# Hyena long convolution: the inverse transform over folded spectra, and the first output tile between the inverse transforms

## The chip, the cores and the metric

One core of a Trainium2 chip runs the whole program in one launch. The metric is the device time in microseconds (us) of that core, median of the runs. The engines named here are TensorE (PE; its weight loads PEld), VectorE (DVE), ScalarE (ACT), GpSimd (POOL) and the queue of SyncE (SP) that starts most transfers.

## The reference, cut to what matters

Four layers over 256 latent and 256 context tokens of width 1024; layer 1 is a Hyena mixer, and the change lies in it alone:

```python
def _bidir_long_conv(u, h_fwd, h_bwd, skip):
    l = u.shape[1]
    n = 2 * l
    filt = jnp.concatenate([h_fwd, jnp.zeros_like(h_fwd[:1]), h_bwd[:0:-1]], axis=0)
    uf = jnp.fft.rfft(u.astype(jnp.float32), n=n, axis=1)
    ff = jnp.fft.rfft(filt, n=n, axis=0)
    y = jnp.fft.irfft(uf * ff[None], n=n, axis=1)[:, :l]
    return (y + u.astype(jnp.float32) * skip.astype(jnp.float32)).astype(u.dtype)

def _hyena_mixer(...):
    u = _dwconv(h @ w_in + b_in, conv_w, conv_b)
    x0, x1, v = jnp.split(u, 3, axis=-1)
    ...
    v = _bidir_long_conv(v * x1, h_fwd, h_bwd, skip)
    return (v * x0) @ w_out + b_out
```

It runs on the latent and on the context tokens with the same weights. Everything is float32.

## The kernel before, in words

The transform is taken at 256 odd frequencies as matrix products. A frequency k and its mirror 255-k are handled as a pair: even and odd input samples are transformed apart (128 frequencies each), and a sum and a difference of the two ("butterfly") give the 256 spectra. The long convolution is cut into four windows w = 0 to 3: w = 2*hf + st, where hf is the half of the 1024 channels and st is latent or context. For each window:

- `turn_x1v(w)` (PE, L1044) turns the gated input by 8 transposes; ACT copies it out.
- `forward(w, im)` (PE, L1060) makes the even and odd parts; ACT copies the odd part (`odd_part`).
- `butterflies(w, im)` (DVE, L1895, L1897): 2 instructions for the real and 2 for the imaginary part.
- `products(w, b)` (DVE, L1909 to L1917): for each half b of the frequencies 4 products and 2 sums, written to `y_spec`; 12 instructions a window.
- `inverse(w)` (PE, L1075): for each of 4 channel blocks 4 float32 products of 128 channels by 256 samples (real and imaginary, b = 0 and 1) into one accumulation. A float32 product is recorded as two MATMUL instructions, so a window has 32.
- `gate(w)` (DVE, L1925): 2 instructions multiply the result, from PSUM, by x0 into `x1v`.
- ACT (L1455) copies it into `u_hi` in 4 pieces, POOL (L2029) makes `u_lo` in 4 pieces and raises `c_lo` at each.

Windows 0 and 1 go through forward and products inside the last four input tiles (t = 8 to 11 of `hyena_in`), where PE is busy with the projection; windows 2 and 3 come after the last one. There DVE's written order is: the products (1,1), then for w = 2 and 3 the butterflies, the products and `gate(w - 2)`, then `gate(2)` and `gate(3)`. PE's is forward(2), inverse(0), turn 3, forward(3), inverse(1), inverse(2), inverse(3), and then the output projection `x_phase`. `products(w, 0)` of w = 2 and 3 waits for inverse(w - 2), as it writes over its `y_spec`.

The output projection has four weight tiles. Its first one (t = 0) takes channels 0 to 511, which are windows 0 and 1, for 4 blocks of 128 tokens: per block a bias product and 12 MATMULs. Before the first of these it waits for `c_lo` of 8. The second tile takes channels 512 to 1023 and waits for `c_lo` of 16. The weights of a tile are loaded by SP once the tile three before is done, and split into `w_hi` (ACT L1155) and `w_lo` (DVE L1517). Each engine runs its list in order; waits are on semaphores, set by hand.

Of the kernel before, what the change touches and what calls it, by code (L numbers as in the profile page):

```python
# [21 lines left out]
P = 128  # L22
# [77 lines left out]
def constants():  # L100

    f = np.float32
    out = {}

    def rope(dh):
        axis = dh // 2
        inv = np.power(f(10000.0), -np.arange(0, axis, 2, dtype=f) / f(axis)).astype(f)
        t = np.arange(SEQ)
        ang = np.concatenate([(t // GRID_W).astype(f)[:, None] * inv[None],
                              (t % GRID_W).astype(f)[:, None] * inv[None]], axis=-1)  # L110
        half = dh // 2
        cos, sin = np.zeros((P, SEQ), f), np.zeros((P, SEQ), f)
        for p in range(P):
            cos[p] = np.cos(ang[:, p % half]).astype(f)
            sin[p] = np.sin(ang[:, p % half]).astype(f)

        rot = np.zeros((P, P), f)
        for p in range(P):
            if p % dh < half:
                rot[p + half, p] = -1.0  # L120
            else:
                rot[p - half, p] = 1.0
        return cos, sin, rot

    cos, sin, rot = rope(A_DH)
    out["k_rope_a"] = np.concatenate([cos, sin, rot], axis=1)
    cos, sin, rot = rope(C_DH)

    mats = [rot]
    for kv in range(C_KV):  # L130
        dup = np.zeros((P, P), f)
        for p in range(P):
            dup[C_DH * kv + p % C_DH, p] = 1.0
        mats += [dup, (rot.astype(np.float64) @ dup).astype(f)]
    mask = np.zeros((2, P, TOK), f)
    for b in range(2):
        q = b * P + np.arange(P)[:, None]
        mask[b, :, :SEQ] = np.where(np.abs(np.arange(SEQ)[None, :] - q) <= 128, 0.0, -1e30)
    out["k_rope_c"] = np.concatenate([cos, sin] + mats + [mask[0], mask[1]], axis=1)

    pick = np.zeros((P, 2), f)
    for p in range(P):
        if p % 32 < 2:
            pick[p, p % 32] = 1.0
    out["k_ident"] = np.concatenate([np.eye(P, dtype=f), 1.0 - np.eye(P, 1, dtype=f), pick], axis=1)


    t = np.linspace(0.0, 1.0, SEQ, dtype=f)[:, None]
    omega = (f(2.0 * math.pi / SEQ) * np.arange(SEQ, dtype=f)).astype(f)
    bands = np.linspace(1e-4, 15, 16, dtype=f)  # L150
    ang = (omega[:, None] * bands[None, :]).astype(f)
    z = np.concatenate([t, np.cos(ang), -np.sin(ang)], axis=-1).astype(f)
    out["k_zt"] = np.ascontiguousarray(z.T)
    rates = np.abs(np.linspace(math.log(1e-2) / 0.3, math.log(1e-2) / 1.5, D, dtype=f))
    by_parity = np.concatenate([np.arange(0, SEQ, 2), np.arange(1, SEQ, 2)])
    out["k_decay"] = np.exp(-t * rates[None, :]).astype(f)[by_parity]

    pos = np.arange(SEQ, dtype=np.float64)[:, None]
    th = 2 * np.pi * ((pos * (2 * np.arange(SEQ)[None, :] + 1)) % (2 * NFREQ)) / (2 * NFREQ)
    out["k_dft"] = np.concatenate([np.cos(th[:, :P]), -np.sin(th[:, :P])], axis=1)[by_parity].astype(f)

    order = np.concatenate([np.arange(P), SEQ - 1 - np.arange(P)])
    ang = th.T[order]
    out["k_idft"] = (2.0 / NFREQ * np.concatenate([np.cos(ang), -np.sin(ang)], axis=0)).astype(f)
    return out


def build(nc, a, out):

    es = ExitStack()
    with es:
# [67 lines left out]
        def region(*items):  # L242

            got, at = [], M0
            for name, shape, off in items:
# [21 lines left out]
            ("decay", [P, 2, D], None), ("f_w4", [P, D], None), ("f_w", [P, 4 * FW], None), ("f_b", [P, 3], None))  # L267
        ZT, SK = region(("f_in", [P, SEQ], 4 * 16 * TOK), ("skip_row", [P, D], None))
        YS, VX, IF = region(("y_spec", [P, 2, 4, 512], 4 * (16 * TOK + 5 * D + 12 * P)),
                            ("x1v_tok", [P, 2, 2, 512], None), ("idft", [P, 4, SEQ], None))  # L270

        MG = [None] * 4
        MG += region(*((f"mod_unit{s}", [P, KT, TW], 8 * D * (s - 4)) for s in range(4, 8)))
# [6 lines left out]
        def rope_mat(m):  # L280
# [44 lines left out]
        f_odd, c_odd = sem("f_odd"), sem("c_odd")  # L325
        c_turned, c_vt, c_fwd, c_fly, c_prod, c_y = (sem("c_turned"), sem("c_vt"), sem("c_fwd"), sem("c_fly"),
                                                     sem("c_prod"), sem("c_y"))
        c_inv, c_gated, c_hi, c_lo = sem("c_inv"), sem("c_gated"), sem("c_hi"), sem("c_lo")
        dve_chain = sem("dve_chain")

# [252 lines left out]
        def _(pe):  # L583
# [129 lines left out]
                                  start=True, stop=True)  # L713
                    last.then_inc(u_turned, 1)

            def x_phase(k, X, Y, arrive, free):

                n0, nt, NB = XFIRST[k], XTILES[k], XN[k]
                kts = [sum(TILES[n0 + t][3] for t in range(x)) for x in range(nt)]
# [23 lines left out]
                for t in range(2 * nt - 2):  # L743
                    n, (h, tt) = n0 + t, divmod(t, nt)
                    nr, kt = TILES[n][3], kts[tt]
                    pe.wait_ge(lo_ready, n + 1)
                    if k % 2 == 0 and tt == 1:
                        for j in range(nr):
                            arrive(kt + j)
                            for b in range(NB):  # L750
                                ins = step(n, h, b, j, kt, False, j == nr - 1)
                                if j == nr - 1:
                                    finished(h, b, ins)
                            if j == nr // 2 - 1:
                                for x in MID.get(n, []):
                                    reduce_mod(x)
                    else:
                        for b in range(NB):
                            if tt == 0:
                                enter(h, b)  # L760
                            for j in range(nr):
                                if h == 0 and b == 0:
                                    arrive(kt + j)
                                ins = step(n, h, b, j, kt, not has_bias(k) and tt == 0 and j == 0, tt == nt - 1 and j == nr - 1)
                            if tt == nt - 1:
                                finished(h, b, ins)
                            if b == NB // 2 - 1:
                                for x in MID.get(n, []):
                                    reduce_mod(x)
                    ins.then_inc(tile_done, 1)  # L770
                    for x in END.get(n, []):
                        reduce_mod(x)

# [289 lines left out]
            def long_conv():  # L1063
                def inverse(w):
                    pe.wait_ge(c_y, 4 * (w + 1))
                    if w == 0:
                        pe.wait_ge(tab_in, TAB_AT[1] + 16)
                        pe.wait_ge(c_fly, 8)
                    elif w == 1:
                        pe.wait_ge(c_vt, 8)  # L1070
                    else:
                        pe.wait_ge(c_gated, 2 * (w - 1))
                    for c in range(4):
                        for j in range(4):
                            last = mm(y_bank(w, c // 2)[:, (c % 2) * SEQ:(c % 2 + 1) * SEQ], YS[:, w % 2, j, c * P:(c + 1) * P],  # L1075
                                      IF[:, j, :], start=(j == 0), stop=(j == 3))
                    last.then_inc(c_inv, 1)

                def spectra(w):
                    forward(w, 0)  # L1080
                    forward(w, 1)

                spectra(2)
                inverse(0)
                turn_x1v(3)
                spectra(3)
                inverse(1)
                inverse(2)
                inverse(3)

            for i in range(DEPTH):
                N = NL[i]
                n0, q0 = FIRST["in", i], PAIR0["in", i]
                if KIND[i] == 1:
# [3 lines left out]
                    for t in range(2, 12):  # L1098
# [5 lines left out]
                        if t in (8, 10):  # L1104
                            forward(t // 2 - 4, 0)
                            forward(t // 2 - 4, 1)
                    long_conv()
                    arrive = lambda k: pe.wait_ge(c_lo, 8 * (k // 4 + 1))
                    free = lambda b: ((c_fly, 16),)
                else:  # L1110
                    if i > 0:
                        first_tiles(n0, q0, 2 * i, (N, TOK))
                    issued = 0 if KIND[i] == 2 else 3 if i == 0 else 4
# [18 lines left out]
                    arrive = lambda k, G=ahead(GROUPS, i): pe.wait_ge(ao_lo, G + k + 1)  # L1132
                    free = lambda b, i=i: ((p_evac, ahead(NH, i) + NH[i]),) if b < 2 else ((ao_lo, ahead(GROUPS, i) + GROUPS[i] - 3 + b),)

                x_phase(2 * i, UH, UL, arrive, free)

                n0, q0 = FIRST["up", i], PAIR0["up", i]
                first_tiles(n0, q0, 2 * i + 1, (N, N))
# [362 lines left out]
        def _(dve):  # L1501
# [319 lines left out]
            def hyena_in():  # L1821
# [4 lines left out]
                for t in range(12):  # L1826
# [47 lines left out]
                        butterflies(t // 2 - 4, 1)  # L1874
                    if t >= 8:
                        products(t // 2 - 4, t % 2)

            def filter_taps(x):

# [19 lines left out]
            def products(w, b):  # L1899
# [12 lines left out]
                tt(re, im, BF[:, 2 + b, s], ALU.mult).then_inc(c_prod, 1)  # L1912
                tt(im, im, BF[:, b, s], ALU.mult).then_inc(c_prod, 1)
                dve.wait_ge(c_prod, n + 3)
                tt(y_re, y_re, re, ALU.subtract).then_inc(c_y, 1)
                dve.wait_ge(c_prod, n + 4)
                tt(y_im, y_im, im, ALU.add).then_inc(c_y, 1)  # L1917

            def long_conv():
                def gate(w):  # L1920
                    hf, st = divmod(w, 2)
                    dve.wait_ge(c_inv, w + 1)
                    for m in range(2):
                        cs, t = slice(4 * hf + 2 * m, 4 * hf + 2 * m + 2), slice(st * SEQ, (st + 1) * SEQ)
                        tt(XV[:, cs, t], y_bank(w, m).rearrange("p (c t) -> p c t", c=2), X0[:, cs, t],  # L1925
                           ALU.mult).then_inc(c_gated, 1)

                dve.wait_ge(z_conv, 3 * KT)
                for w in (2, 3):
                    butterflies(w, 0)  # L1930
                    butterflies(w, 1)
                    products(w, 0)
                    products(w, 1)
                    gate(w - 2)
                gate(2)
                gate(3)

# [202 lines left out]
```

## Time and profile before

| | |
|---|---|
| median of 3 runs | 2210.0 us (2206.38 to 2210.42) |
| profiled execution | 2205.8 us, of which the span is 2204.0 us |
| PE busy | 2133.3 us, 97% of the span |
| DVE busy | 1447.3 us, 66% |
| ACT busy | 888.9 us, 40% |
| POOL busy | 187.0 us, 8% |
| mean granted PE clock | 0.993 |

Times in the views are counted from the start of the span. A busy share is an average over the whole program; the long convolution outside the input tiles is the stretch from 812 to 851.8 us of it. MATMULs are pipelined, so the pitch from start to start is what a stream of them costs, and their recorded durations overlap.

### The profile page before, as it was taken

To read this page: it belongs to the slowest core of one execution; us is meant where nothing else is said; L and a number is where in the kernel's file an instruction comes from. 1 tells how busy PE (TensorE), PEld (TensorE's weight loads), DVE (VectorE), ACT (ScalarE), POOL (GpSimd) and SP (SyncE) were. 2 spreads that over 40 slices of the span, in tenths; PEclk is the share of its full clock that TensorE was granted. 3 is DMA by queue.
4 is the path that set the end of the run, shared out by engine and by line. 5 is a ranking of instruction groups with operands and counts; after the bars stand their busy time and mean duration, and the time that the engine had idled before them with its cause. 6 is when DMAs were issued, how large, how long until landed. Compare 5 with 4: busy or idle time off the path is not lost.

```text
span 2204.0 us, 28517 instructions
## 1 busy us (share of the span) xinstructions
PE 2133.3 (97%) x11580; PEld 1746.1 (79%) x11580; DVE 1447.3 (66%) x2195; ACT 888.9 (40%) x1345; POOL 187.0 (8%) x222
## 2 busy tenths in 40 slices
PE   6999999999999999999999998999999999998998
PEld 4767888888787777988888796588888878868996
DVE  2426557878766675678877656855787785656554
ACT  3336443332243442533332245844333224355543
POOL 0000011111010002011110011101111100100110
PEclk9999999999999999999999999999999999999999
DMA  9650335546542222245546531022555653214554
GB/s 316 195 173 20 115 105 163 170 155 215 186 141 77 87 76 77 77 135 162 172 153 220 172 106 58 21 91 91 162 161 166 198 194 124 84 49 149 174 192 143
DMA packets 224696, 304.44 MB, mean 138 GB/s; under 512 B 6762, under 2 KB 153259, under 8 KB 224438
## 3 DMA queue, kind: packets, MB, share of 16 engines
q1 hardware_dynamic: 220537, 290.11, 40.5%
q0 software_dynamic: 3632, 12.35, 1.7%
q8 instruction: 92, 1.51, 0.3%
q14 instruction: 38, 0.31, 0.0%
q10 hardware_dynamic: 397, 0.15, 0.0%
HBM read 301.48 MB, written 1.11 MB: 137 GB/s over the span
## 4 chain that ended last, share of the span: by engine, by line
PE 84%; DVE 8%; ACT 4%; DMA 2%; issue 1%; SPq 0%; POOL 0%; ACTq 0%; DVEq 0%; POOLq 0%
PE lo L658 17%; PE lo L659 16%; PE lo L660 16%; PE lo L724 4%; PE lo L725 4%; PE lo L726 4%; PE hi L724 2%; PE hi L726 2%; PE hi L725 2%; PE lo L955 2%; DVE w_lo L1517 1%; ACT w_hi L1155 1%; DMA w_raw<-in_ffn_w_down 1%; PE stat L724 1%; PE modp L624 1%
## 5 line engine op out<-in xcount | busy, mean ns | idle before, releaser
L658 PE MATMUL lo<-u_hi,w_hi 128*128 128x512 f32 (+1 forms) x2016 | 717.5, 356 | 5.0 <-DVE w_lo L1517 4.5
L659 PE MATMUL lo<-u_lo,w_hi 128*128 128x512 f32 (+1 forms) x2016 | 704.9, 350 | 0.0
L660 PE MATMUL lo<-u_hi,w_lo 128*128 128x512 f32 (+1 forms) x2016 | 704.6, 350 | 0.0
L1517 DVE TENSOR_TENSOR w_lo<-w_raw,w_hi 128x2048 fp32r<-128x2048 f32 (+1 forms) x182 | 406.4, 2234 | 337.1 <-ACT w_hi L1155 335.7
L1155 ACT ACTIVATE w_hi<-w_raw 128x2048 fp32r<-128x2048 f32 (+1 forms) x182 | 339.8, 1868 | 480.7 <-DMA w_raw<-in_ffn_w_down 259.8
L658 PEld LDWEIGHTS lo<-u_hi,w_hi 128*128 128x128 f32 x2016 | 382.6, 190 | 67.7 <-issue 18.7
L660 PEld LDWEIGHTS lo<-u_hi,w_lo 128*128 128x128 f32 x2016 | 382.4, 190 | 49.6
L659 PEld LDWEIGHTS lo<-u_lo,w_hi 128*128 128x128 f32 x2016 | 382.7, 190 | 49.0 <-issue 1.2
L1534 DVE SCALAR_TENSOR_TENSOR mod_acc<-mod_raw,silu_c,mod_acc 128x512 f32<-128x512 f32 x504 | 394.5, 848 | 7.2 <-DMA mod_raw<-in_mod_w 7.2
L2079 POOL TENSOR_TENSOR mid_lo<-conv,mid_hi 128x512 fp32r<-128x512 f32 (+1 forms) x88 | 117.7, 1358 | 1057.4 <-ACT mid_hi L1496 1057.4
L724 PE MATMUL lo<-w_hi,mid_hi 128*128 128x512 f32 x374 | 147.5, 394 | 3.4 <-DVE u_raw L1608 2.5
L725 PE MATMUL lo<-w_lo,mid_hi 128*128 128x512 f32 x374 | 145.8, 390 | 0.0
L726 PE MATMUL lo<-w_hi,mid_lo 128*128 128x512 f32 x374 | 145.6, 389 | 0.0
L1485 ACT ACTIVATE conv<-lo,par 128x512 f32<-128x512 f32 (+1 forms) x88 | 58.8, 719 | 147.4 <-PE lo L660 147.4
L1496 ACT ACTIVATE mid_hi<-conv 128x512 fp32r<-128x512 f32 (+1 forms) x88 | 46.6, 576 | 156.4 <-DVE conv L1974 156.4
L1960 DVE SCALAR_TENSOR_TENSOR conv<-lo,par,conv 128x510 f32<-128x510 f32 (+1 forms) x88 | 56.3, 680 | 62.4 <-ACT conv L1485 62.4
L724 PEld LDWEIGHTS lo<-w_hi,mid_hi 128*128 128x128 f32 x374 | 70.2, 188 | 21.4 <-issue 5.5
L726 PEld LDWEIGHTS lo<-w_hi,mid_lo 128*128 128x128 f32 x374 | 70.2, 188 | 14.9
L725 PEld LDWEIGHTS lo<-w_lo,mid_hi 128*128 128x128 f32 x374 | 70.2, 188 | 14.0
L1490 ACT ACTIVATE conv<-conv 128x512 f32<-128x512 f32 (+1 forms) x88 | 50.7, 579 | 71.4 <-DVE conv L1965 70.7
L1974 DVE TENSOR_TENSOR conv<-conv,lo 128x512 f32<-128x512 f32 (+1 forms) x88 | 50.6, 616 | 24.4 <-PE lo L660 24.3
L955 PE MATMUL lo<-ident,probs 128*128 128x128 f32 x352 | 57.0, 290 | 9.9 <-DVE probs L1782 9.7
(381 smaller groups left out, 2686.9 us busy)
## 6 DMA issues: line engine op xcount, KB each, us to landing
w_raw<-in_ffn_w_up SPq DMA_DIRECT2D x88, 1024.0 KB, 5.1
mod_raw<-in_mod_w SPq DMA_DIRECT2D x144, 512.0 KB, 3.9
w_raw<-in_ffn_w_down SPq DMA_DIRECT2D x40, 1024.0 KB, 5.0
mod_unit<-in_mod_w SPq DMA_DIRECT2D x24, 1024.0 KB, 6.4
w_raw<-in_a_w_qkv SPq DMA_DIRECT2D x12, 1024.0 KB, 5.5
w_raw<-in_b_w_in SPq DMA_DIRECT2D x12, 1024.0 KB, 5.1
w_raw<-in_a_w_out SPq DMA_DIRECT2D x8, 1024.0 KB, 5.0
w_raw<-in_ffn_w_down SPq DMA_DIRECT2D x8, 512.0 KB, 3.6
```

The source lines that it names most:

```text
L658: mm(o, h3[:, k, c], x, start=(first and k == 0), stop=False)
L659: mm(o, h3[:, k, c], y, start=False, stop=False)
L660: ins = mm(o, l3[:, k, c], x, start=False, stop=(last and k == nr - 1))
L724: mm(o, X[:, kt + j, s], h3[:, j, :], start=first, stop=False)
L725: mm(o, X[:, kt + j, s], l3[:, j, :], start=False, stop=False)
L726: return mm(o, Y[:, kt + j, s], h3[:, j, :], start=False, stop=last)
L955: last = nc.tensor.transpose(t_bank(i, x)[:, at * P:(at + 1) * P], p[:, src:src + P], ident)
L1155: f(WH[:, n % 3, 0:words], RAW[:, n % 3, 0:words], ACT.Copy).then_inc(hi_ready, 1)
L1485: f(CV[:, m, 0:N], bank[2 * ((q0 + 2 * s) % 2) + m][:, 0:N], ACT.Identity, scale=col("ffn_conv_w", (3 * i + 1) * FM + c), bias=col("ffn_co ...
L1517: tt(WL[:, n % 3, 0:words], RAW[:, n % 3, 0:words], WH[:, n % 3, 0:words].bitcast(F32), ALU.subtract).then_inc(lo_ready, 1)
L1534: stt(acc, MR[:, k % 2, j, :], S2[:, s:s + 1], acc, ALU.mult, ALU.add).then_inc(mod_step, 1)
L2079: tt(ML[:, c, 0:N], CV[:, c % 2, 0:N], MH[:, c, 0:N].bitcast(F32), ALU.subtract).then_inc(ml_ready, 1)
```

## The change

The sums and differences that the inverse transform needs are made before it: for even output samples Re0+Re1 and Im0-Im1, for odd ones Re0-Re1 and Im0+Im1 (0 and 1 are the frequency halves b). The inverse then runs over 128 frequencies, on 128 samples at a time. `folds(w)` makes them on DVE with 4 instructions of 128x512 a window. `products` leaves its two sums in place of the data's spectrum, not in `y_spec`, and raises the new semaphore `c_sum`; `c_y` is raised by the folds. The result in PSUM has the even samples first and the odd ones behind them, so `gate` reads x0 and writes `x1v` at every second element. `k_idft` is half as large. In DVE's order `gate(1)` stands ahead of the products of window 3. On PE `inverse(2)` and `inverse(3)` stand behind the first tile of the output projection (`between`).

```diff
-    order = np.concatenate([np.arange(P), SEQ - 1 - np.arange(P)])
-    ang = th.T[order]
+    ang = th.T[:P, by_parity]
...
-                            ("x1v_tok", [P, 2, 2, 512], None), ("idft", [P, 4, SEQ], None))
+                            ("x1v_tok", [P, 2, 2, 512], None), ("idft", [P, 2, SEQ], None))
...
-            def x_phase(k, X, Y, arrive, free):
+            def x_phase(k, X, Y, arrive, free, between=None):
...
                     ins.then_inc(tile_done, 1)
+                    if t == 0 and between:
+                        between()
...
                     for c in range(4):
-                        for j in range(4):
-                            last = mm(y_bank(w, c // 2)[:, (c % 2) * SEQ:(c % 2 + 1) * SEQ], YS[:, w % 2, j, c * P:(c + 1) * P],
-                                      IF[:, j, :], start=(j == 0), stop=(j == 3))
+                        for e in range(2):
+                            o = y_bank(w, c // 2)[:, (c % 2) * SEQ + e * P:(c % 2) * SEQ + (e + 1) * P]
+                            for j in range(2):
+                                last = mm(o, YS[:, w % 2, 2 * j + e, c * P:(c + 1) * P], IF[:, j, e * P:(e + 1) * P],
+                                          start=(j == 0), stop=(j == 1))
...
                 inverse(1)
-                inverse(2)
-                inverse(3)
+
+                def rest():
+                    inverse(2)
+                    inverse(3)
+                return rest
...
-                x_phase(2 * i, UH, UL, arrive, free)
+                x_phase(2 * i, UH, UL, arrive, free, between)
...
                     if t >= 8:
                         products(t // 2 - 4, t % 2)
+                    if t in (9, 11):
+                        folds(t // 2 - 4)
...
-                tt(y_re, y_re, re, ALU.subtract).then_inc(c_y, 1)
+                tt(re, y_re, re, ALU.subtract).then_inc(c_sum, 1)
                 dve.wait_ge(c_prod, n + 4)
-                tt(y_im, y_im, im, ALU.add).then_inc(c_y, 1)
+                tt(im, y_im, im, ALU.add).then_inc(c_sum, 1)
+
+            def folds(w):
+
+                dve.wait_ge(c_sum, 4 * w + 4)
+                for part, ops in ((0, (ALU.add, ALU.subtract)), (2, (ALU.subtract, ALU.add))):
+                    for e in range(2):
+                        tt(YS[:, w % 2, part + e, :], spectrum(w, part), spectrum(w, part + 1), ops[e]).then_inc(c_y, 1)
...
-                        tt(XV[:, cs, t], y_bank(w, m).rearrange("p (c t) -> p c t", c=2), X0[:, cs, t],
-                           ALU.mult).then_inc(c_gated, 1)
+                        x, x0 = [z[:, cs, t].rearrange("p c (n e) -> p c e n", e=2) for z in (XV, X0)]
+                        tt(x, y_bank(w, m).rearrange("p (c e n) -> p c e n", c=2, e=2), x0, ALU.mult).then_inc(c_gated, 1)
...
                 for w in (2, 3):
                     butterflies(w, 0)
                     butterflies(w, 1)
+                    if w == 3:
+                        gate(1)
                     products(w, 0)
                     products(w, 1)
-                    gate(w - 2)
+                    folds(w)
+                    if w == 2:
+                        gate(0)
                 gate(2)
                 gate(3)
```

## Rows read from the trace of the kernel before

**Rows 1.** The page: PE's busy time, the chain's shares, a DVE group, a weight load.
```profile
PE 2133.3 (97%) x11580; PEld 1746.1 (79%) x11580; DVE 1447.3 (66%) x2195; ACT 888.9 (40%) x1345; POOL 187.0 (8%) x222
...
PE 84%; DVE 8%; ACT 4%; DMA 2%; issue 1%; SPq 0%; POOL 0%; ACTq 0%; DVEq 0%; POOLq 0%
...
L658 PEld LDWEIGHTS lo<-u_hi,w_hi 128*128 128x128 f32 x2016 | 382.6, 190 | 67.7 <-issue 18.7
...
L1534 DVE SCALAR_TENSOR_TENSOR mod_acc<-mod_raw,silu_c,mod_acc 128x512 f32<-128x512 f32 x504 | 394.5, 848 | 7.2 <-DMA mod_raw<-in_mod_w 7.2
```

**Rows 2.** Chain of waits, 790 to 900 us: start us, us, what.
```profile
816.50 6.91 PE hi L1075 x32
...
835.69 0.69 DVE y_spec L1909
...
843.26 1.21 DVE x1v L1925 x2
844.60 3.69 PE stat L1075 x16
```

**Rows 3.** Timeline of PE: start us, us, instructions, idle before them and its releaser.
```profile
851.40 0.58 PE L737 MATMUL lo<-bias_split,two_ones 128*128 128x512 f32 x1
851.82 0.39 PE L724 MATMUL lo<-w_hi,u_hi 128*128 128x512 f32 x1
...
863.50 0.39 PE L724 MATMUL lo<-w_hi,u_hi 128*128 128x512 f32 x1
...
874.38 0.39 PE L737 MATMUL stat<-bias_split,two_ones 128*128 128x512 f32 x1
```

**Rows 4.** Timeline of PE, float32 products of 128 columns in the next stage.
```profile
891.50 1.05 PE L712 MATMUL stat<-conv,h 128*128 128x128 f32 x8
892.38 1.06 PE L712 MATMUL hi<-conv,h 128*128 128x128 f32 x8
```

**Rows 5.** Timeline of DVE, 798 to 833 us.
```profile
798.53 0.75 DVE L1840 SCALAR_TENSOR_TENSOR x<-conv,par,x 128x510 f32<-128x510 f32 x1 [2.95 <-ACT x L1419]
...
816.76 0.69 DVE L1909 TENSOR_TENSOR y_spec<-squares,filter_spec 128x512 f32<-128x512 f32 x1
...
820.49 0.68 DVE L1895 TENSOR_TENSOR data_spec<-lo,data_spec 128x512 f32<-128x512 f32 x1
821.21 0.69 DVE L1897 TENSOR_TENSOR data_spec<-lo,data_spec 128x512 f32<-128x512 f32 x1
821.82 0.68 DVE L1895 TENSOR_TENSOR data_spec<-lo,data_spec 128x512 f32<-128x512 f32 x1
...
823.45 0.69 DVE L1909 TENSOR_TENSOR y_spec<-data_spec,filter_spec 128x512 f32<-128x512 f32 x1 [0.22 <-PE hi L1075]
...
830.93 1.28 DVE L1925 TENSOR_TENSOR x1v<-hi,x 128x512 f32<-128x512 f32 x2
832.13 0.68 DVE L1895 TENSOR_TENSOR v_conv<-lo,squares 128x512 f32<-128x512 f32 x1
```

**Rows 6.** Timelines of DVE, ACT and POOL: from the last gate to c_lo.
```profile
851.78 0.69 DVE L1925 TENSOR_TENSOR x1v<-stat,x 128x512 f32<-128x512 f32 x1 [6.13 <-PE modp L1075]
...
852.51 1.34 ACT L1455 ACTIVATE u_hi<-x1v 128x256 fp32r<-128x256 f32 x4 [6.06 <-DVE x1v L1925]
...
853.01 2.83 POOL L2029 TENSOR_TENSOR u_lo<-x1v,u_hi 128x256 fp32r<-128x256 f32 x4 [3.10 <-ACT u_hi L1455]
```

**Rows 7.** Windows: length, then PE, PEld, DVE, ACT, POOL busy, PEclk, DMA share, GB/s.
```profile
677.00:678.00 1.00, 1.00 (x4) 0.80 (x3) 0.54 (x1) 1.00 (x2) 0.00 (x0) 0.50 0.08 16
...
844.00:846.00 2.00, 1.40 (x7) 1.27 (x8) 1.65 (x3) 2.00 (x7) 1.61 (x3) 1.00 0.00 0
```

**Rows 8.** Timeline of PE around the idle time of rows 7.
```profile
675.68 0.64 PE L1006 MATMUL hi<-f_act,f_w 64*64 64x256 f32 x2 [2.88 <-ACT f_act L1424]
...
676.84 0.63 PE L660 MATMUL lo<-u_hi,w_lo 128*128 128x512 f32 x1
...
680.23 0.39 PE L659 MATMUL lo<-u_lo,w_hi 128*128 128x512 f32 x1
```

More of the change, by code:

```diff
@@ L327, in build @@
                                                      sem("c_prod"), sem("c_y"))
+        c_sum = sem("c_sum")
         c_inv, c_gated, c_hi, c_lo = sem("c_inv"), sem("c_gated"), sem("c_hi"), sem("c_lo")
@@ L1106, in _ @@
                             forward(t // 2 - 4, 1)
-                    long_conv()
+                    between = long_conv()
                     arrive = lambda k: pe.wait_ge(c_lo, 8 * (k // 4 + 1))
@@ L1110, in _ @@
                 else:
+                    between = None
                     if i > 0:
```

## The prediction

> **What bounds the kernel now.** I read the page first: PE is busy for 97% of the span, and the chain that ended last lies on PE for 84% of it, on DVE for 8% [rows 1]. So a delay of PE in this stage reaches the end nearly one to one, and a saving counts only where PE, not DVE, is what the stage waits for. The chain of waits through the stage says which. It runs on PE through inverse(0), 6.91 us for 32 instructions, on PE again through inverse(1), then from 835.69 to 844.5 on DVE (the products of window 3 and gate(1)), then through inverse(3) on PE [rows 2]. So the stage changes hands: the inverse transforms of windows 0, 1 and 3 stand on the path, and that of window 2 lies beside DVE's products. DVE's timeline shows how near it is behind: from 816.76 to 835 it works without a gap of more than 0.22 us [rows 5]. Its products of window 2 start 0.22 us after PE released them; DVE has no room to take on work here without setting the end itself. That is the question of this change, for it moves work from PE to DVE.
>
> The figure to beat is the start of the second tile of the output projection, 863.50 us [rows 3], the first point behind which all order is as before.
>
> **The change part by part.**
>
> The inverse transform. Before, 32 instructions of 256 columns take 6.91 us, 0.216 each [rows 2]. After, 32 of 128 columns. The same form, a float32 product of 128 columns with a new 128x128 weight for each, stands in the next stage: 8 of them from 891.50 to 892.38, 0.110 each [rows 4]. So 32 take 3.5 us, and four windows give PE back 13.5 us. The bounds of the pitch: 0.108 (half of 0.216), and 0.190, the duration of one weight load [rows 1], if the loads did not overlap. I take 0.110, because rows 4 have the very form.
>
> The folds. Four DVE instructions a window of 128x512 float32. The first depends on the instruction before it: the pitch of a dependent pair is 821.21 - 820.49 = 0.72, that of an independent one 821.82 - 821.21 = 0.61 [rows 5]. So a window takes 4*0.605 + 0.11 = 2.53 us. Bounds: 0.60 to 0.72 an instruction, by those two, or 2.4 to 2.9 us. For window 0 they come after the products (0,1) in input tile 9, where DVE idles 2.95 us before L1840 at 798.53 [rows 5]: hidden, with 0.4 us left. Were that cover gone, the input tile's taps and the tiles behind them would be late by what exceeds it. For windows 1, 2 and 3 nothing hides them; DVE has no gap.
>
> The gates. Two instructions, 1.20 us from 830.93 to 832.13 [rows 5]. They now read x0 and write x1v at every second element, and no row shows that on DVE. Below, 0.60 an instruction as now; above, 0.85, the slowest 128x512 float32 form on the page (L1534) [rows 1]. It is the same operation on as many elements, so I take 0.60; the upper end adds 0.5 in gate(0), 0.25 in gate(1) and 0.25 in gate(3) on the path, 1.0 in all. Less than nothing is excluded, since the elements are as many. On this the Trainium skill has a rule (SBUF — State Buffer, section "Specifications (TRN2)", its row on cachelines): a line of 16 bytes must be hit at least twice for full bandwidth, which a step of two float32 words just does. By it the addition is nil, by the upper row 1.0 us; no run shows it yet.
>
> The second half of `k_idft` that isn't loaded is off the path. The tab_in wait of inverse(0) was long met; I cost it at nothing.
>
> The DVE chain, which I lay out from 816.76, the products (1,1), as before [rows 5]:
> - products (1,1): 820.49 - 816.76 = 3.73, to 820.49
> - folds(1): 2.53, to 823.02
> - butterflies of window 2: 0.72 + 0.61 + 0.72 + 0.60 = 2.65, to 825.67. Their input was ready at 820.49
> - products of window 2: 830.93 - 823.45 = 7.48, to 833.15. inverse(0), for which they wait, ends near 820
> - folds(2): 2.53, to 835.68
> - gate(0): 1.20, to 836.88
> - butterflies of window 3: 2.65, to 839.53. They need forward(3). That waits for the butterflies of window 2 to clear its banks, starts at 824.5, and ends near 828.3
> - gate(1) starts at 839.5. Before it started at 843.26 [rows 2]. inverse(1) is over by 832, so it waits for nothing.
>
> So gate(1), moved ahead of the products of window 3, is only 3.7 us earlier. What it passes, the products (7.48) and folds(3) (2.53), then runs to 850.7.
>
> From a gate to the release of the projection: DVE 851.78, ACT 852.51, POOL 853.01 + 2.83 = 855.84, so 4.06 us, and 0.1 for PE to take it [rows 6]. POOL sets it, with four pieces at 0.7. Hence `c_lo` reaches 8 and PE starts the first output tile at 839.5 + 4.16 = 843.7. PE's own queue is empty from about 832 (one bias product apart): 12 us of idle time, where the saved 13.5 us have gone.
>
> Then it is serial. The first tile without its first bias: 863.50 - 851.82 = 11.7 us [rows 3], to 855.4. Behind it are queued inverse(2) and inverse(3), whose input has been ready since 850.7: 2*3.5 = 7.0, to 862.4. gate(3) starts 0.38 after the stream, as at 851.78 [rows 6] after the bias product that followed that stream at 851.40 [rows 3]. Then 4.16 us through ACT and POOL as above, with PE idle: the second tile starts at 862.4 + 0.38 + 4.16 = 866.9. Before, that chain after gate(3) was covered by the first output tile; moving the tile ahead of inverse(2) and (3) takes this cover away. Against 863.50 the stage is later by 3.4 us.
>
> Behind the moved tile: the load of the fourth weight tile starts when the first is done, some 8 us earlier; w_hi and w_lo of the third wait on ACT and DVE behind gate(3) and its copies, until about 869, and that of the fourth until about 876. PE wants them at 878 and 881. Nothing is late there, and nothing gained.
>
> The clock. An idle time of 2.88 us before 675.68 [rows 8] is followed by a granted clock of 0.50, which is 1.2 of 2.4 GHz [rows 7]. From 676.84 to 680.23 PE issues 8 instructions at 0.42 instead of 0.227: 3.39 - 1.82 = 1.6 us lost [rows 8]. The idle time of 2.04 before 844.60 left the clock at 1.00 [rows 7]. The changed kernel has two idle times on the path, of 12 and of 4.5 us, each followed by a dense tile, so I take 1.6 us twice, 3.2. The bounds are 0 and 2*1.9. The Trainium skill (TensorE: Matmul & The Clock Gate, "Why this matters for your kernels") speaks against this change in the same way: a TensorE left idle between bursts falls back to the half clock and must work at it before it is released. By that rule both idle times cost as in rows 8; were it the other way, the stage would come out at 3.4 alone. A third idle time, about 3.4 us before forward(3), may halve the clock there too. That delays inverse(1) to about 834, still ahead of gate(1): nothing.
>
> Sum: +3.4 + 3.2 = +6.6 us. Against the profiled execution's 2205.8 (span 2204.0) that is 2212.4; the median of the runs shown stands 4.2 above it, so 2216.6. I round to 2216.5.
>
> **The rivals.**
>
> Clock kept (+3.4, 2213.4). The same order, but the halved clock falls mainly on idle time, or the second idle time is too short for it. For it: rows 7 show one idle time of 2 us that cost nothing. Against: both new ones are well above the 2.88 us that did.
>
> Dearer instructions (+8 to +12, about 2219). The strided gate at its upper end adds 1.0. A pitch of 0.190 in inverse(2) and (3) adds 2*32*0.08 = 5.1. Rows 4 speak against the latter.
>
> Faster, the PE bound. If gate(1) were not held by DVE, PE would go from inverse(1), which its own queue ends at about 829 (turn 3, forward(3), then 3.5 us), straight into the first tile. That ends at 841, inverse(3) at 848, and the second tile starts near 852.6, 11 us sooner than now: 2199. The place is gate(1), and each us by which it starts before 839.5 gives one back. It decides for faster once gate(1) starts before 833, or 836 if the clock is kept. It would need DVE's 22.8 us from 816.76 to be shorter by nearly a third; the rows give every one of its instructions but the folds and gates, and they are what they are now. In part it might hold, say 2204.
>
> No effect (2210). Some of the delay is taken up later, in waits for weights. PE sits nowhere in this projection, so I find no place for it.
>
> **How the numbers follow.** Forecast 0.55, with 2214 to 2219 as its own range; clock kept 0.20; dearer 0.10; faster 0.09; no effect 0.06. The range is 2208 to 2221: it takes in the clock kept, most of "dearer" and the scatter of the medians (4 us among three runs), and leaves out the faster case. A measurement of this kernel can tell 0.2%, 4.4 us, from no change. Slower by more: nearly all of the forecast and of "dearer", 0.60. Within: the clock kept, no effect and the low edge of the forecast, 0.31. Faster: 0.09.
>
> **What would show it.** L1075 at a pitch of 0.11; four folds in 2.5 us; gate(1) starting at 839.5 and PE idle for about 12 us before the first output tile; inverse(3) ending at 862 to 864, another 4 to 5 us of idle time, and the second tile at 867 to 869; a PEclk of 0.50 behind both idle times. It is wrong if gate(1) comes before 836, if the first output tile starts before 841, if L1075 keeps a pitch near 0.2, or if PEclk stays 1.00 throughout.

## The result and the profile after

The changed kernel takes 2217.9 us against 2209.0 (medians of 13 runs each), ratio 1.0043, 95% interval 1.0034 to 1.0052. It is slower by 8.9 us, where 6.6 were forecast. Its profiled span is 2214.2 us against 2204.0.

To compare traces whose starts differ by some us, I measure one stage: from the start of forward(2) behind the last input tile (812.10 before) to the first bias product of the second column half (874.38, the last of [rows 3]). It took 62.3 us before and takes 71.7 now, 9.4 more. So nearly all of the span's 10.2 lies in this stage; 0.2 lies ahead of it and 0.6 behind it.

The timeline of PE through the stage in the changed kernel (L1062 is forward, L1079 inverse, L737 the bias product, L724 the output projection); it answers to [rows 3]:

```profile
812.32 1.88 PE L1062 MATMUL lo<-x1v_tok,dft 128*128 128x512 f32 x4
...
816.56 3.73 PE L1079 MATMUL hi<-idft,y_spec 128*128 128x128 f32 x32
...
824.80 6.47 PE L1062 MATMUL lo<-x1v_tok,dft 128*128 128x512 f32 x8 [3.55 <-DVE data_spec L1907]
831.11 1.95 PE L1079 MATMUL stat<-idft,y_spec 128*128 128x128 f32 x16
832.89 1.95 PE L1079 MATMUL modp<-idft,y_spec 128*128 128x128 f32 x16
839.92 0.76 PE L737 MATMUL lo<-bias_split,two_ones 128*128 128x512 f32 x1 [5.07 <-issue]
845.64 0.80 PE L724 MATMUL lo<-w_hi,u_hi 128*128 128x512 f32 x1 [4.96 <-POOL u_lo L2050]
...
859.89 3.73 PE L1079 MATMUL hi<-idft,y_spec 128*128 128x128 f32 x32
863.46 1.95 PE L1079 MATMUL stat<-idft,y_spec 128*128 128x128 f32 x16
865.24 1.95 PE L1079 MATMUL modp<-idft,y_spec 128*128 128x128 f32 x16
871.37 0.74 PE L724 MATMUL lo<-w_hi,u_hi 128*128 128x512 f32 x1 [4.18 <-POOL u_lo L2050]
...
883.97 0.39 PE L737 MATMUL stat<-bias_split,two_ones 128*128 128x512 f32 x1
```

The inverse did become as short as hoped: 863.46 - 859.89 = 3.57 us for 32 instructions against 6.91 [rows 2]. The four windows return 13.4 us, and PE spends more than that waiting: 3.6 us before forward(3), 10.8 us with one bias product in them between inverse(1) and the first tile (834.84 to 845.64), 4.2 us before the second. Before, its two waits of this kind were 0.70 and 2.04 us.

The timeline of DVE, which answers to [rows 5] (L1919 to L1927 are the products and their sums, L1934 the folds, L1905 and L1907 the butterflies, L1943 the gates):

```profile
793.63 2.50 DVE L1934 TENSOR_TENSOR y_spec<-data_spec 128x512 f32<-128x512 f32 x4
...
798.75 0.75 DVE L1848 SCALAR_TENSOR_TENSOR x<-conv,par,x 128x510 f32<-128x510 f32 x1 [0.43 <-ACT x L1427]
...
820.83 2.50 DVE L1934 TENSOR_TENSOR y_spec<-v_conv,squares 128x512 f32<-128x512 f32 x4
823.25 0.68 DVE L1905 TENSOR_TENSOR data_spec<-lo,data_spec 128x512 f32<-128x512 f32 x1
...
833.48 2.50 DVE L1934 TENSOR_TENSOR y_spec<-data_spec 128x512 f32<-128x512 f32 x4
835.89 1.28 DVE L1943 TENSOR_TENSOR x1v<-hi,x 128x512 f32<-128x512 f32 x2
837.09 0.68 DVE L1905 TENSOR_TENSOR v_conv<-lo,squares 128x512 f32<-128x512 f32 x1
...
839.73 0.68 DVE L1943 TENSOR_TENSOR x1v<-stat,x 128x512 f32<-128x512 f32 x1
...
840.93 0.68 DVE L1919 TENSOR_TENSOR y_spec<-v_conv,filter_spec 128x512 f32<-128x512 f32 x1
841.53 1.21 DVE L1920 TENSOR_TENSOR y_spec<-v_conv,filter_spec 128x512 f32<-128x512 f32 x1
842.77 1.10 DVE L1922 TENSOR_TENSOR v_conv<-v_conv,filter_spec 128x512 f32<-128x512 f32 x1
843.79 1.21 DVE L1923 TENSOR_TENSOR v_conv<-v_conv,filter_spec 128x512 f32<-128x512 f32 x1
844.92 1.21 DVE L1925 TENSOR_TENSOR v_conv<-y_spec,v_conv 128x512 f32<-128x512 f32 x1
846.05 0.68 DVE L1927 TENSOR_TENSOR v_conv<-y_spec,v_conv 128x512 f32<-128x512 f32 x1
```

The folds of window 0 left 0.43 us of DVE's slack. From 816.98 to 853 DVE has no gap. The strided gates cost nothing: 835.89 to 837.09 is 1.20 us for two, as before. But four instructions of the first half of the products, 841.53 to 846.05, take 1.1 to 1.2 us instead of 0.68. POOL's timeline has the counterpart, its second row against the others and against [rows 6]:

```profile
837.12 2.77 POOL L2050 TENSOR_TENSOR u_lo<-x1v,u_hi 128x256 fp32r<-128x256 f32 x4 [108.86 <-ACT u_hi L1463]
840.94 4.64 POOL L2050 TENSOR_TENSOR u_lo<-x1v,u_hi 128x256 fp32r<-128x256 f32 x4 [1.06 <-ACT u_hi L1463]
...
868.45 2.77 POOL L2050 TENSOR_TENSOR u_lo<-x1v,u_hi 128x256 fp32r<-128x256 f32 x4 [0.79 <-ACT u_hi L1463]
```

The granted clock in windows of the changed kernel (columns as in [rows 7]; PEclk is the third figure from the end):

```profile
849.00:850.00 1.00, 1.00 (x3) 0.78 (x3) 1.00 (x3) 0.00 (x0) 0.00 (x0) 0.50 0.00 0
...
851.00:852.00 1.00, 1.00 (x6) 0.82 (x5) 1.00 (x3) 0.00 (x0) 0.00 (x0) 1.00 0.00 0
...
873.00:874.00 1.00, 1.00 (x3) 0.77 (x3) 1.00 (x3) 0.00 (x0) 0.00 (x0) 0.50 0.01 1
...
875.00:876.00 1.00, 1.00 (x6) 0.81 (x5) 1.00 (x2) 0.00 (x0) 0.97 (x2) 1.00 0.00 0
```

In both output tiles PE is busy all the time, first at 0.50, half the full clock, and then at 1.00.

### The profile page after: what moved, and what is told of

It reads as the page before. It is cut to its first block, busy times and chain, and to the rows that moved or that the text cites. A ratio compares the mean times of both kernels' runs of the same rounds, so it can differ in the third digit from the quotient of the medians.

```text
span 2214.2 us, 28533 instructions
## 1 busy us (share of the span) xinstructions
PE 2128.7 (96%) x11580; PEld 1740.5 (79%) x11580; DVE 1459.1 (66%) x2211; ACT 888.8 (40%) x1345; POOL 188.2 (9%) x222
## 4 chain that ended last, share of the span: by engine, by line
PE 83%; DVE 8%; ACT 4%; DMA 2%; issue 1%; POOL 0%; SPq 0%; ACTq 0%; DVEq 0%; POOLq 0%
PE lo L658 17%; PE lo L659 16%; PE lo L660 16%; PE lo L724 4%; PE lo L725 4%; PE lo L726 4%; PE hi L724 2%; PE hi L726 2%; PE hi L725 2%; PE lo L957 2%; DVE w_lo L1525 1%; ACT w_hi L1163 1%; DMA w_raw<-in_ffn_w_down 1%; PE stat L724 1%; PE modp L624 1%
## 5 line engine op out<-in xcount | busy, mean ns | idle before, releaser
L724 PE MATMUL lo<-w_hi,mid_hi 128*128 128x512 f32 x374 | 147.5, 394 | 3.5 <-DVE u_raw L1616 2.7
L724 PEld LDWEIGHTS lo<-w_hi,mid_hi 128*128 128x128 f32 x374 | 70.2, 188 | 21.6 <-issue 5.7
```

The costliest lines, as they stand in the source:

```text
L724: mm(o, X[:, kt + j, s], h3[:, j, :], start=first, stop=False)
```

## The experiments

My theory has four parts: DVE holds gate(1); the moved tile uncovers the ACT and POOL stretch behind gate(3); both idle times cost the clock; and, seen only in the trace of after, POOL and DVE slow each other. Rivals: the new order is the gain and only the folds cost; POOL's 4.6 us has another cause; the long tiles have another cause than the clock.

The stage in all traces, in us:

| kernel | stage | against before | measured ratio to before (95%) |
|---|---|---|---|
| before | 62.3 | | |
| changed | 71.7 | +9.4 | 1.0043 (1.0034 to 1.0052) |
| e1_order_back | 69.4 | +7.1 | 1.0024 (1.0013 to 1.0034) |
| e2_order_only | 74.8 | +12.5 | 1.0053 (1.0041 to 1.0066) |
| e3_pool_alone | 69.4 | +7.1 | 1.0028 (1.0017 to 1.0039) |
| e4_mid_tile | 65.6 | +3.4 | 1.0009 (1.0000 to 1.0018) |
| e5_kept_warm | 67.8 | +5.5 | 1.0022 (1.0013 to 1.0032) |
| e6_mixed | 56.2 | -6.0 | 0.9966 (0.9953 to 0.9979) |
| e7_long_mid | 60.0 | -2.3 | 0.9982 (0.9972 to 0.9993) |
| e8_one_fold | 57.9 | -4.4 | 0.9977 (0.9968 to 0.9986) |
| e9_mixed_in_row | 64.1 | +1.8 | 1.0001 (0.9991 to 1.0011) |

A ratio of 0.001 is 2.2 us, so between neighbours of the table the traces decide. Each stage is read from one trace. For all nine variants the measured ratio gives 0.6 to 1.8 us less than the stage does (e6_mixed: -7.5 against -6.0); each of these gaps is within the interval, but they all point one way, and what lies outside the stage is not explained.

**The order taken back.**

```diff
 # the changed kernel
                 inverse(1)
-                def rest():
-                    inverse(2)
-                    inverse(3)
-                return rest
+                inverse(2)
+                inverse(3)
```

> The changed kernel with inverse(2) and inverse(3) ahead of the output projection again; the folded inverse and DVE's order stay. My theory (DVE's chain is the bound, and the moved tile only uncovers the ACT and POOL stretch after gate(3)): PE idles from about 839.6 until folds(3) are done near 853, inverse(3) ends at 857 to 860 (its clock may be halved), the first output tile follows at once and covers gate(3); the second tile starts near 870 and ends near 881, 3 us before the changed kernel's 884.0. So 3 us less than the changed kernel and 6 to 7 us more than before, ratio to before 1.003. Rival (the order is the gain of the change and only the folds cost): it is slower than the changed kernel, 3 us or more over it, ratio 1.006.

Measured: 2215.1 us; the stage is 2.3 us shorter than the changed kernel's. Its PE timeline shows the wait that takes the other's place:

```profile
837.00 5.31 PE L1079 MATMUL hi<-idft,y_spec 128*128 128x128 f32 x32 [2.58 <-DVE x1v L1940]
852.73 3.79 PE L1079 MATMUL stat<-idft,y_spec 128*128 128x128 f32 x16 [10.43 <-DVE y_spec L1931]
856.31 2.38 PE L1079 MATMUL modp<-idft,y_spec 128*128 128x128 f32 x16
858.45 0.48 PE L737 MATMUL lo<-bias_split,two_ones 128*128 128x512 f32 x1
```

PE waits 10.4 us for folds(3), and inverse(3) takes 5.7 (852.73 to 858.45), as the granted clock is 0.50 until about 857. The rival is out: PE's new order is no gain. But with PE's old order the folded inverse is 7.1 us over before too. Not all of that is the price of the folds, for this variant keeps gate(1) ahead of the products, where POOL slows DVE as in the changed kernel: the four slowed instructions take 4.52 us from the first start to the next one's behind them (841.21 to 845.73), against 2.53 in the kernel before (836.30 to 838.83). That is 2.0 us of DVE's path, which leaves an estimated 5 us for the folds. No run has the folds with both old orders.

**The order alone, on the kernel before.**

```diff
 # the kernel before, with between() as in the change
                     butterflies(w, 1)
+                    if w == 3:
+                        gate(1)
                     products(w, 0)
                     products(w, 1)
-                    gate(w - 2)
+                    if w == 2:
+                        gate(0)
```

> The kernel before with the new order alone (first output tile ahead of inverse(2) and (3), gate(1) ahead of the products of window 3); the inverse over 256 frequencies, no folds, contiguous gates. My theory: gate(1) starts at 836.0, held by inverse(1), c_lo reaches 8 near 842 if POOL is slowed as in the changed kernel (840 if not), and inverse(2), inverse(3) and the uncovered 4.2 us stand behind the first tile: the second starts near 874 and ends near 887. That is 12 to 13 us over before, ratio 1.0057. Rival (the order is harmless and the folds cost it all): within 2 us of before, ratio 1.000 to 1.001.

Measured: 2220.0 us, the stage 12.5 us over before, as forecast. The order alone is a loss, larger than that of the whole change. With the order given, folding takes 3.1 us back. The two parts don't add: each turns PE's time into a wait for the same chain. In the second tile the clock costs more here than in the changed kernel, behind the same idle time of 4.18 us:

```profile
876.64 0.76 PE L724 MATMUL lo<-w_hi,u_hi 128*128 128x512 f32 x1 [4.18 <-POOL u_lo L2038]
```

```profile
877.00:881.00 4.00, 4.00 (x10) 3.08 (x10) 4.00 (x6) 1.16 (x1) 0.83 (x2) 0.50 0.04 8
...
882.00:883.00 1.00, 1.00 (x5) 0.81 (x4) 1.00 (x3) 0.00 (x0) 0.00 (x0) 0.68 0.85 242
```

The second tile runs at half the clock for 5.9 us, not 3.4, and takes 13.8 us, not 12.6.

**POOL left alone.**

```diff
 # the changed kernel
                     if w == 3:
                         gate(1)
+                        dve.wait_ge(c_lo, 8)
                     products(w, 0)
```

> The changed kernel, with one more wait: DVE starts the products of window 3 only when POOL has finished u_lo of window 1 (c_lo of 8). Theory (DVE instructions that read both operands from SBUF and POOL slow each other down): POOL's four pieces take 2.8 us and not 4.6, the first output tile starts 1.8 us earlier, DVE's L1920 to L1925 are back at 0.68, and folds(3) end at 854, still ahead of the end of the first tile. So 1.8 us less than the changed kernel. Rival (POOL's 4.6 has another cause, or a longer DVE delay takes the gain): no difference, or 3 us more.

Measured: 2215.6 us, the stage 2.3 us shorter than the changed kernel's, where 1.8 were expected. POOL's and DVE's timelines:

```profile
842.21 2.77 POOL L2051 TENSOR_TENSOR u_lo<-x1v,u_hi 128x256 fp32r<-128x256 f32 x4 [108.89 <-ACT u_hi L1463]
846.04 2.76 POOL L2051 TENSOR_TENSOR u_lo<-x1v,u_hi 128x256 fp32r<-128x256 f32 x4 [1.06 <-ACT u_hi L1463]
```

```profile
848.83 0.69 DVE L1919 TENSOR_TENSOR y_spec<-v_conv,filter_spec 128x512 f32<-128x512 f32 x1 [2.72 <-POOL u_lo L2051]
849.44 0.68 DVE L1920 TENSOR_TENSOR y_spec<-v_conv,filter_spec 128x512 f32<-128x512 f32 x1
```

An added wait makes the stage shorter (the ratios of the whole, 1.0028 and 1.0043, have intervals that overlap, so this rests on the traces). From gate(1) to the first MATMUL on its result it is 4.0 us (844.83 to 848.86) where the changed kernel has 5.9. That is 1.9 of the 2.3 us; the other 0.4 are shorter stretches of half clock in the two tiles. This shows that the overlap is the cause of POOL's 4.6. Which operands matter no run isolates, but the traces show it side by side. In the changed kernel, POOL's first group, 837.12 to 839.9, lies beside butterflies, which read one operand from PSUM, and neither side is slowed; its second lies beside products with both operands in SBUF. In the kernel before, eight pieces beside gates, which read one operand from PSUM, take 0.69 us each:

```profile
844.39 5.52 POOL L2029 TENSOR_TENSOR u_lo<-x1v,u_hi 128x256 fp32r<-128x256 f32 x8 [9.45 <-ACT u_hi L1455]
```

The Trainium skill states the rule (SBUF — State Buffer, "Who interferes with whom"): a VectorE instruction with two SBUF inputs contends with a GpSimd one that reads SBUF, because its second input comes through a read interface that the two share; one with at most one SBUF input does not, outside VectorE's 2-port modes. The traces of the changed kernel (4.64 us) and of e3_pool_alone (2.76) agree.

**The inverses inside the tile.**

```diff
 # the changed kernel, x_phase
                         for b in range(NB):
                             ...
+                            if t == 0 and b == 1 and between:
+                                between()
                     ins.then_inc(tile_done, 1)
-                    if t == 0 and between:
-                        between()
```

> The changed kernel with inverse(2) and (3) behind the second of the four token blocks of the first output tile, not behind the fourth. Theory (the uncovered stretch after gate(3) and the clock lost in it): inverse(3) ends near 861.2, blocks 3 and 4 cover gate(3), ACT and POOL, the second tile starts near 867.1 instead of 871.4 without an idle time ahead of it and at the full clock. So 6 us less than the changed kernel (4.3 of wait, 1.7 of clock), some 3.5 us over before, ratio 1.0016. Rival (the wait is taken over by something else, such as folds(3) not being ready): less than 2 us gained.

Measured: 2210.8 us; the stage is 6.0 us shorter than the changed kernel's, as forecast. Token blocks 3 and 4 now cover gate(3), ACT and POOL. Behind inverse(3) PE goes on at once:

```profile
859.56 1.95 PE L1079 MATMUL modp<-idft,y_spec 128*128 128x128 f32 x16
861.27 0.48 PE L737 MATMUL lo<-bias_split,two_ones 128*128 128x512 f32 x1
```

The second tile then starts at 867.32 without a wait, at a granted clock of 1.00, and takes 10.9 us. The uncovered stretch and its clock cost are shown together: 4.2 us of wait and 1.7 of clock make 5.9 of the 6.0.

**Products that nobody reads.**

```diff
 # the changed kernel, PE
                 inverse(1)
+                def filler(n):
+                    for _ in range(n):
+                        mm(bank[6], TWO[:, :], BS[:, 0:HW], start=True, stop=True)
+                pe.wait_ge(c_gated, 2)
+                pe.wait_ge(b_lo, 1)
+                filler(26)
                 def rest():
                     inverse(2)
                     inverse(3)
+                    pe.wait_ge(c_gated, 6)
+                    filler(16)
```

> The changed kernel with products added that nobody reads: 26 MATMULs of 512 columns after gate(0) while PE waits for c_lo of 8, and 16 after inverse(3) while it waits for 16. Theory (the halved clock behind both idle times costs 2.6 and 1.7 us): the granted clock is back at 1.00 before both output tiles, they take 11.7 and 10.9 us instead of 14.3 and 12.6, and the run takes 4.3 us less than the changed kernel. Rival (the tiles are longer for another reason than the clock, or the fillers delay them): no difference, or 1 to 2 us more.

Measured: 2211.8 us; the stage is 3.9 us shorter than the changed kernel's (4.3 expected), with 42 MATMULs more (L1095):

```profile
837.88 7.79 PE L1095 MATMUL hi<-bias_split,two_ones 128*128 128x512 f32 x26 [2.30 <-DVE x1v L1953]
845.51 0.39 PE L737 MATMUL lo<-bias_split,two_ones 128*128 128x512 f32 x1
846.34 0.50 PE L724 MATMUL lo<-w_hi,u_hi 128*128 128x512 f32 x1 [0.45 <-POOL u_lo L2060]
...
858.20 3.73 PE L1079 MATMUL hi<-idft,y_spec 128*128 128x128 f32 x32
```

Windows at the start of both tiles show a granted clock of 1.00:

```profile
846.00:850.00 4.00, 3.66 (x16) 2.98 (x17) 3.96 (x7) 0.00 (x0) 0.29 (x1) 1.00 0.00 0
...
870.00:875.00 5.00, 5.00 (x23) 4.10 (x23) 5.00 (x7) 1.21 (x1) 1.35 (x3) 1.00 0.35 140
```

The first tile takes 858.20 - 846.34 = 11.9 us and not 14.3, the second 11.0 and not 12.6. The clock's price is 4 us. It did fall here too, to 0.50 from about 838.1 to 841.5, but then PE ran products that nobody waits for.

**A version meant to be faster.** Fold only window 0, where DVE has room, and window 3, whose short inverse stands on PE's path, and put inverse(3) in the middle of the first tile. The unfolded windows use the full table, its columns sorted by parity, so that all gates are alike.

```diff
 # the changed kernel, with b == 1 as in e4_mid_tile
+FOLDED = (0, 3)
...
-    ang = th.T[:P, by_parity]
+    order = np.concatenate([np.arange(P), SEQ - 1 - np.arange(P)])
+    ang = th.T[order][:, by_parity]
...
                     for c in range(4):
+                        if w not in FOLDED:
+                            for j in range(4):
+                                last = mm(y_bank(w, c // 2)[:, (c % 2) * SEQ:(c % 2 + 1) * SEQ],
+                                          YS[:, w % 2, j, c * P:(c + 1) * P], IF[:, j, :], start=(j == 0), stop=(j == 3))
+                            continue
...
                 inverse(1)
+                inverse(2)
                 def rest():
-                    inverse(2)
                     inverse(3)
...
+                to = (re, im, c_sum) if w in FOLDED else (y_re, y_im, c_y)
-                tt(re, y_re, re, ALU.subtract).then_inc(c_sum, 1)
+                tt(to[0], y_re, re, ALU.subtract).then_inc(to[2], 1)
...
             def folds(w):
+                if w not in FOLDED:
+                    return
...
```

> A version meant to be faster than both: folds and the short inverse for windows 0 and 3 alone, the inverse over 256 frequencies for windows 1 and 2 (full table, even samples first), inverse(2) ahead of the output projection, inverse(3) behind the second token block of its first tile. Theory: without folds(1) and folds(2) gate(1) starts near 834.9, c_lo reaches 8 at 839 to 841, PE has inverse(1) and (2) to do until 839.6 and hardly idles; inverse(3) ends near 851.6; the second tile starts near 857.6 against 863.5 before. So 6 us less than before, ratio 0.997. Rival (the stage is bound by PE's sum of work or by another wait, so shorter inverses give nothing): within 2 us of before.

Measured: 2198.9 us against 2208.3, the ratio 0.9966 (0.9953 to 0.9979). It is faster than both kernels. The stage is 6.0 us shorter than before's, as forecast. Its PE timeline has no long gap, and the clock stays at 1.00 throughout:

```profile
820.83 3.67 PE L1064 MATMUL lo<-x1v_tok,dft 128*128 128x512 f32 x8 [1.03 <-DVE data_spec L1914]
...
831.24 7.07 PE L1080 MATMUL hi<-idft,y_spec 128*128 128x256 f32 x32
839.15 0.50 PE L726 MATMUL lo<-w_hi,u_hi 128*128 128x512 f32 x1 [0.61 <-POOL u_lo L2060]
846.57 2.05 PE L1086 MATMUL stat<-idft,y_spec 128*128 128x128 f32 x16 [1.42 <-DVE y_spec L1944]
```

**Its parts.** Three variants of e6_mixed say what the 6.0 us are made of.

```diff
-FOLDED = (0, 3)
+FOLDED = ()        # e7_long_mid
+FOLDED = (0,)      # e8_one_fold
 # e9_mixed_in_row: inverse(3) straight behind inverse(2), no rest()
```

> As e6_mixed but no window folded: all four inverses over 256 frequencies with strided gates, inverse(2) ahead of the projection, inverse(3) behind the second block of its first tile, gate(1) ahead of the products of window 3. Theory: inverse(2) ends at 842.8, c_lo reaches 8 by 842, two blocks to 848.6, inverse(3) to 855.5, the second tile starts near 861.4: 2 us less than before, ratio 0.999, and 4 us more than e6_mixed, which is what two short inverses give there. Rival: the folds are worth nothing in any place, e6_mixed and this one are the same.

> As e6_mixed, but only window 0 is folded; window 3 has the inverse over 256 frequencies and no folds. Theory (e6_mixed's gain is made of a fold that is hidden on DVE and a short inverse(3) that stands on PE's path): the sums of window 3 are ready 2.5 us earlier, but PE then hardly waits for them (1.4 us in e6_mixed), and inverse(3) takes 6.9 instead of 3.6. So 2 us more than e6_mixed and 4 us less than before, ratio 0.998. Rival (DVE still decides, so the folds of window 3 cost as much as they save): the same as e6_mixed within 1 us.

> As e6_mixed, but inverse(3) straight behind inverse(2), ahead of the whole output projection. Theory (the placement inside the tile is what keeps PE fed): PE waits about 8 us for folds(3), its clock falls, inverse(3) takes 4 to 6 us and the first tile follows; the second tile starts 9 us later than in e6_mixed: 2 to 3 us over before, ratio 1.001. Rival (the gain of e6_mixed is the smaller sum of work on PE and DVE, wherever it stands): within 2 us of e6_mixed.

Measured: 2204.5, 2202.5 and 2207.0 us. By the stages, the placement in the tile (with gate(1) ahead of the products) gives 2.3 us with no fold at all, folding window 0 gives 2.1 more, folding window 3 another 1.7 (forecast 2, 2 and 2). Without the placement the folds (0, 3) end 1.8 us over before, 7.9 later than e6_mixed: in e9_mixed_in_row PE waits 8.25 us for the folds of window 3. The medians of e7, e8 and e9 have intervals 0.002 wide, so this split rests on the traces. The rival, that the gain is the smaller sum of work wherever it stands, is out.

## Why the prediction was right

It followed DVE's list from 816.76 row by row, and that carries most of the result. The stage of the changed kernel began 0.2 us later than that of before, so 0.2 is to be taken off a start in its trace to compare it with the forecast. Each step beside what was measured:

- The inverse: 3.5 us a window forecast, 3.57 found. The folds: 2.53 and 2.4 to 2.5. The gates at 0.60: found.
- gate(1) at 839.5: found 839.73, less 0.2. PE's queue empty for 12 us: found 10.8, from 834.8 to 845.6 in its trace, with one bias product; inverse(1) ended later than I laid out (834.6, not 832), behind a forward(3) at half the clock.
- From gate(1) to the first tile, 4.16: found 5.91 (839.73 to 845.64), as POOL was slowed. **This term was missing**, 1.75 us. The prediction took POOL's pieces at 0.7 from [rows 6], where DVE stood still beside them. It moved gate(1) ahead of the products and did not ask what POOL would then run beside.
- The first tile, 11.7 us and 1.6 for the clock: found 14.25, so the clock took 2.55. **This term was mis-sized**, by 0.95. In [rows 7, 8] the stream ran on half the clock for some 3.4 us; here the clock came back only between 850 and 851, some 5.2 us after 845.64. My upper bound of 1.9, for which the prediction gives no working, did not hold.
- inverse(2) and (3), 7.0, and gate(3) to the second tile, 4.16: found 7.1 and 4.14.
- The second tile, 10.9 and 1.6 for the clock: found 12.60, so 1.7.

6.6 + 1.75 + 0.95 + 0.1 is 9.4, the difference of the stage. Of the signs that I named, the end of inverse(3) (862 to 864) and the start of the second tile (867 to 869) came later, at 866.8 and 871.2, by these two terms; none of the signs of being wrong appeared. That the time itself, 2216.5, is only 1.4 us from the measured 2217.9 is in part luck: its base of 2210.0 was 1.0 above the later median of the kernel before, which hides part of what the two terms lack. The rival "dearer" is summed wrongly in the prediction: its two additions to 6.6, of 1.0 and 5.1, give 12.7 and not at most 12. The uncovered chain behind gate(3), the step that made the sign plain, is shown by e4_mid_tile; the clock's price by e5_kept_warm; the missing term by e3_pool_alone. The third idle time, before forward(3), halved the clock (forward(3) took 6.3 us and not 3.5) and cost nothing, since inverse(1) was still 5 us ahead of gate(1), as I had said. The rival of a faster kernel required gate(1) well ahead of 839.5. e6_mixed is that case: DVE has two folds fewer before it, gate(1) starts 5.0 us earlier in the stage than in the changed kernel, and the stage is faster. Two things separate the two kernels: which windows are folded, and where inverse(2) and (3) stand. Moving both inverse transforms into the tile gives 6.0 of the 15.4 us (e4_mid_tile); the other 9.4 come with the two folds fewer and inverse(2) ahead of the tile, and no run parts these.

The fourth weight tile was on time: PE waits for nothing from the start of the second tile, 871.37, to 905. One thing came nearer than I wrote: the gate rows that POOL loads after its last piece are now what the view names as the last wait of DVE's first instruction on them (2.52 us, L1616 at 882.91). No delay by it is shown: that instruction starts 0.79 us behind ACT's on the same result, in before (872.53 and 873.32) as now (882.12 and 882.91).

## What to carry to other kernels

Work moved from the busiest engine to another is a gain where the other has a gap (window 0), or where the shorter work behind it stands on the path and saves more than the wait it brings (window 3 in e6_mixed, 1.7 us); decide per instance (here per window), not for the whole loop. When a tile is moved ahead of something, ask what it used to cover: a serial chain through three engines behind a product needs PE work behind that product, so put the product in the middle of the tile. Before an instruction on one engine is moved, look at what the others will then run beside it.

## What was not expected of the hardware

GpSimd's 128x256 float32 tensor operations took 0.70 us each while VectorE stood still or read one operand from PSUM, and 1.16 (4.64 for four) beside VectorE ones with both operands in SBUF; of the five VectorE ones that overlapped them the first still took 0.68 us, the other four 1.1 to 1.2. A wait that keeps them apart made the stage 2.3 us shorter.

After 10.8 us with one MATMUL in them the granted clock stayed at 0.50 for another 5.2 us of the first tile; after 4.2 us of idle time for 3.4 us of the second. But the idle time does not set the length: in e2_order_only the same 4.2 us were followed by 5.9 us at 0.50, and forward(3), behind the same 3.6 us, took 6.3 us in the changed kernel and 5.1 in e3_pool_alone (3.5 at the full clock). What sets it stays open. The idle times of e6_mixed, up to 1.4 us, left the clock at 1.00; in e5_kept_warm one of 2.3 us was followed by 0.50, with PE busy again. I had priced both tiles by the one case of [rows 8].
